# Interleaving the weight units of the gate stage one by one, and converting one unit ahead instead of two

## The reference

```python
mod_x = jax.nn.silu(c) @ ada_w[l] + ada_b[l]                     # c: (1, 1024), ada_w: 1024 x 6144
sh1, sc1, g1, sh2, sc2, g2 = jnp.split(mod_x[:, None, :], 6, axis=-1)
...
px = hx @ w_in[l]                                                # gates gx: 2048 of its columns
g = jax.nn.sigmoid(gates + b_gate)
y = g_f * (f_mix @ w_fourier) + g_a * (att @ w_mla_o)
x = x + g1 * (y @ w_out)
```

## Time and profile before

| | us |
|---|---|
| median of three runs | 1771.61 |
| the profiled execution, its own time | 1770.47 |
| its span in the profile | 1768.7 |
| PE busy | 1677.0 (95%) |
| DVE busy | 1200.7 (68%) |
| ACT busy | 871.0 (49%) |
| the gate stage on PE, about | 151 to 247 |

### The profile page before, as it was taken

One profiled execution on the slowest core, in us unless ns is written; L12 is line 12 of the kernel. 1 busy time (PEld: TensorE's weight loads), 2 busy tenths in 40 slices (PEclk: granted clock), 3 DMA queues, 4 the chain that ended last, 5 costly groups with the idle time before them and its releaser, 6 DMA issues.

```text
span 1768.7 us, 18457 instructions
## 1 busy us (share of the span) xinstructions
PE 1677.0 (95%) x7530; PEld 1307.9 (74%) x7530; DVE 1200.7 (68%) x1334; ACT 871.0 (49%) x973; POOL 112.8 (6%) x139
## 2 busy tenths in 40 slices
PE   5999998989899999998999999889999999999994
PEld 2768875658688888886787667768888888888882
DVE  6545857776553434344487675489898989999894
ACT  6423234443342323232533124467888787887872
POOL 0000021000000000000000220020101011110100
PEclk8999998999899999998999998889999999999997
DMA  9106730012122222221221100279999999999983
GB/s 382 57 31 264 271 111 1 0 48 95 72 96 95 96 95 96 96 95 48 96 75 69 48 25 30 96 265 365 374 373 380 371 359 366 361 371 368 382 326 154
DMA packets 54522, 322.77 MB, mean 182 GB/s; under 512 B 12577, under 2 KB 13089, under 8 KB 17826
## 3 DMA queue, kind: packets, MB, share of 16 engines
q1 hardware_dynamic: 42480, 305.81, 45.9%
q0 software_dynamic: 9216, 8.42, 1.4%
q10 hardware_dynamic: 2738, 7.33, 1.1%
HBM read 325.70 MB, written 20.97 MB: 196 GB/s over the span
## 4 chain that ended last, share of the span: by engine, by line
PE 87%; DVE 8%; ACT 2%; DMA 2%; issue 1%; POOL 0%; SPq 0%; DVEq 0%; POOLq 0%; ACTq 0%
PE ps L524 34%; PE ps L1275 18%; PE ps L1302 10%; PE ps L640 3%; PE ps L1164 2%; PE ps L859 2%; PE ps L1261 2%; DVE scr L2242 2%; DVE wlo L1932 1%; PE ps L925 1%; PE ps L673 1%; PE ps L1004 1%; PE ps L962 1%; DMA xT<-in_x 1%; PE ps L743 1%
## 5 line engine op out<-in xcount | busy, mean ns | idle before, releaser
L1932 DVE TENSOR_TENSOR wlo<-raw,whi 128x2048 fp32r<-128x2048 f32 x268 | 606.7, 2284 | 170.2 <-ACT whi L1363 170.0
L1363 ACT ACTIVATE whi<-raw 128x2048 fp32r<-128x2048 f32 x268 | 508.5, 1914 | 208.6 <-PE ps L524 103.2
L524 PE MATMUL ps<-hH,whi 128*128 128x512 f32 x576 | 229.4, 398 | 0.0
L524 PE MATMUL ps<-hL,whi 128*128 128x512 f32 x576 | 227.5, 395 | 0.0
L524 PE MATMUL ps<-hH,wlo 128*128 128x512 f32 x576 | 227.4, 395 | 0.0
L1275 PE MATMUL ps<-whi,xH 128*128 128x512 f32 x512 | 204.2, 399 | 0.0
L1275 PE MATMUL ps<-whi,xL 128*128 128x512 f32 x512 | 201.2, 393 | 0.0
L1275 PE MATMUL ps<-wlo,xH 128*128 128x512 f32 x512 | 200.0, 391 | 0.0
L524 PEld LDWEIGHTS ps<-hH,whi 128*128 128x128 f32 x576 | 108.1, 188 | 26.3 <-issue 0.5
L524 PEld LDWEIGHTS ps<-hH,wlo 128*128 128x128 f32 x576 | 108.1, 188 | 26.2
L524 PEld LDWEIGHTS ps<-hL,whi 128*128 128x128 f32 x576 | 108.2, 188 | 26.1 <-issue 0.5
(11 more groups left out here) (478 smaller groups left out, 2639.8 us busy)
## 6 DMA issues: line engine op xcount, KB each, us to landing
raw<-in_experts SPq DMA_DIRECT2D x192, 1024.0 KB, 7.4
raw<-in_streamed SPq DMA_DIRECT2D x92, 1024.0 KB, 4.8
xT<-in_x SPq DMA_DIRECT2D x1, 2048.0 KB, 17.2
h_scratch<-hN ACTq DMA_DIRECT2D x4, 512.0 KB, 3.3
Y<-y_scratch SPq DMA_DIRECT2D x4, 512.0 KB, 7.8
Y<-y_scratch ACTq DMA_DIRECT2D x4, 512.0 KB, 8.1
out<-xN SPq DMA_DIRECT2D x4, 512.0 KB, 2.6
ctxT<-in_ctx SPq DMA_DIRECT2D x1, 1024.0 KB, 18.7
```

What stands on the lines that cost most here:

```text
L524: ins = e.matmul(o, l, r, start=(i == 0), stop=(i == len(prs) - 1))
L1363: e.activation(u.hi, u.raw, ACT.Copy).then_inc(*p.inc("hi", n, on="hi"))
L1932: e.tensor_tensor(u.lo, u.raw, u.hi.bitcast(F32), ALU.subtract).then_inc(*p.inc("lo", n, on="lo"))
```

## The change

In the list of units, the order before was g0, g1, mod 4 (two units), g2, mod 5 (two), g3, and so on to g7, mod 10, mod 11. Now it is g0, mod 4, g1, mod 5, g2, and so on to g7, mod 11. In iteration i of the gate stage ACT and DVE converted unit g(i+2); now they convert g(i+1), and on DVE this comes ahead of `mod_row(4 + i)` instead of behind it.

```diff
@@ unit_table
-    for i in range(9):
-        if i < 8:
-            wide("g", "w_in", 0, 8, 928 + 256 * i, 1184 + 256 * i)
-        if i:
-            mod(3 + i)
+    for i in range(8):
+        wide("g", "w_in", 0, 8, 928 + 256 * i, 1184 + 256 * i)
+        mod(4 + i)
@@ act_program, stage "gates"
             use(n)
-            if i + 2 < len(U_G):
-                convert(U_G[i + 2])
+            if i + 1 < len(U_G):
+                convert(U_G[i + 1])
             for m in (2 * i, 2 * i + 1):
                 p.wait_ge(*done("pe", "g", m))
```

## The result

The changed kernel took 1801.88 us, median of 4 runs (1798.51 to 1805.34), against 1771.24 us for the kernel before on the same chip (4 runs, 1770.47 to 1772.28). By these medians it is 30.6 us slower. The ratio of the two kernels is 1.0179, 95% interval 1.0163 to 1.0196; it rests on all 11 runs on record of the changed kernel (1798.51 to 1805.61, mean 1802.95), which is why it is a little above the ratio of the two medians. 1800.5 was predicted. The profiled execution took 1802.24 us.

What follows compares the result with a forecast made beforehand. PE bounded the gate stage before; the change closes a 17.72 us cycle against PE's 12.10. Delay 27.4 + clock 1.5 + end 0.1 = +29.0 us, giving 1800.5 us; 8-in-10 range 1794 to 1807.

Steps and rivals of the forecast that it cites:

- What bounds it: Gate stage before the change: PE never waits and needs 12.10 us per gate unit.
- The ring: Gate stage: row, load, ACT rounding, DVE subtraction, next row form a closed cycle of 17.72 us against PE's 12.10.
- The lag: From a row's end on DVE to the gate unit's landing: 7.5 us, bounds 5.05 and 9.3.
- The start: First gate units: g2 lands at 169.5 us, is ready at 173.8, and PE has 0.7 us to spare.
- The pauses: PE waits ahead of g3 to g7: about 4.9 us ahead of g3, 4 to 5 us ahead of the others.
- The clock: PE at half speed after every pause, losing 1.5 us; only the loss behind g7 stays on the path.
- The end: g7 begins at 262.4 us, row 11 ends just when PE asks, `mod_total(11)` ends at 277.5 against 248.54.
- The sum: Whole kernel: 27.4 + 1.5 + 0.1 = +29.0 us, giving 1800.5 us.
- Loads side by side: Rival: a row's second mod unit and the gate unit load in parallel, lag 5.05 us, 1785.9 us; chance 6%.
- Slower landings: Rival: every gate unit's load lands late, lag 9.3 us, 10.8 us more, 1811 us; chance 5%.
- Clock at half for whole units: Rival: PE runs g3 to g7 at half clock, 21.4 us per unit, 1823 us; chance 3%.
- Not slower: Rival: gate loads go out once their own place is free, no closed cycle, PE bounds, 1771.6 us; chance 4%.

Runs made afterwards that it cites:

- experiment 2: Kernel before with its old load list, but from g2 on converting one gate unit ahead, on DVE ahead of the row: 1772.08 us, ratio 1.0001.
- experiment 3: Changed kernel with DVE's subtraction of g(i+1) moved back behind row 4 + i: 1772.79 us, ratio 1.0001.
- experiment 6: Kernel before with two more DVE multiply-adds in each row: 1771.36 us, ratio 0.9995.
- experiment 1: Changed kernel with its new load list, but gate units converted two ahead again, on DVE behind the row: 1809.71 us, ratio 1.0209.
- Experiment 4: Changed kernel with each gate unit's load placed between the two mod units of a row instead of behind both: 1784.64 us, ratio 1.0071.
- Experiment 7: Changed kernel with 16 more matmuls, results overwritten, ahead of PE's wait for each of g3 to g7: 1803.64 us, ratio 1.0166.
- experiment 5: Changed kernel with two more DVE multiply-adds in each row: 1815.97 us, ratio 1.0233.

## Why the prediction was right, and where its terms were off

**What bounds it.** Right: before, PE alone; experiments 2, 3 and 6 changed lead, loads and DVE's work and moved nothing.

**The ring.** Right as a mechanism and in both of its causes (experiments 1 to 3). Row and subtraction are as worked out (6.06 and 2.21 us on the timeline above). The lag, from the end of the row to the landing, was the uncertain term. It measured 7.9, 7.4, 7.9, 7.3, 9.1 and 7.3 us, together 46.8 where 6 x 7.5 = 45.0 was predicted: +1.8. Five of them lie close to the 7.4 to 7.8 that the pairs of the earlier trace rows gave, and one is a slow landing, as that at 215.2 us was. Three lags lie above 7.5, and in each of these turns it was the mod unit ahead that landed late (5.4, 5.4 and 6.4 us after its issue instead of 4.8 to 4.9); the load of g followed it by 2.5 us in every turn. The mean turn was 18.0 us instead of 17.72. Experiment 4 tests the term from the other side: the load released 3.1 us sooner takes the turn to 14.6.

**The start.** g2 landed at 170.0 instead of 169.5 and PE did not have to wait for it (0.3 us to spare instead of 0.7); the first pause came ahead of g3. Right.

**The pauses.** Five, as forecast, of 3.2 to 5.5 us instead of 4 to 5, 20.8 in all.

**The clock.** Right in kind. The first product of g7 took 7.40 us instead of 5.65: 1.75 instead of the 1.5 read from the earlier trace rows. The size is not fixed, though: in experiment 1 the same product lost 2.9 us, and in experiment 4 four pauses of 1.6 to 3.0 us were followed by no loss at all. Experiment 7 shows that the earlier losses are absorbed.

**The end.** g7 began at 264.36 instead of 262.4, and row 11 was done just when PE asked for it:
```profile
275.23 3.11 DVE L1968 SCALAR_TENSOR_TENSOR rst<-raw,sil,rst 128x512 f32<-128x512 f32 x4 [0.59 <-DMA raw<-in_streamed]
```
It ends at 278.34, and `mod_total(11)` begins at 278.66, 0.48 us after the transposes begin, as it did before: the row was in time by 0.3 us. The row's last half had itself waited for its load; a longer row, as in experiment 5, makes this a wait of 2.3 us for `mod_total(11)`.

**The sum.** +31.2 at the marker for +29.0: +1.8 from the lags, +0.2 from a trace that lies that much later before the stage, and +0.3 in g7's products, most of it the clock (the rounding of the terms makes it 2.3 for 2.2). The median is 1801.88 for 1800.5. That the two lie so close owes a little to chance, since the runs of the changed kernel alone spread over 7.1 us.

**The estimate beside the sum.** The prediction also gives a lag of 9.2 us from the 6.15 us and 341 GB/s that the Trainium skill lists for 1 MB ("DMA: Bandwidth & Descriptors", Measured). These two figures do not fit each other, since 1 MB at 341 GB/s is 3.1 us, and the table is headed as one of transfers issued from GpSimd, where here SP issues them. The lag measured 7.3 to 7.9 us in five turns and 9.1 in one; the sum did not use the estimate.

**The rivals.** Loads side by side (lag 5.05): refuted by all six loads. Slower landings (9.3 each time): one of six (9.1). Clock at half for whole units: refuted by the windows, 1.00 again from 198 us on. Not slower: its condition, a landing within 1.9 us of the row's end, never came near.

## What to carry to other kernels

Two reorderings that are each free can close a ring together, so ask of such a change not what each step costs but whether a unit's release, load and conversion now all lie between one step of an in-order engine and its next. The length of that ring against the bound engine's period gives the time in a sum of four terms, each of which could be read or bounded from the trace before. Then look for the cheapest place to open it: here one step of DVE behind the row instead of ahead of it restored the whole 31 us, and one unit moved in the list 20 us of it.

## What was not expected of the hardware

- Two 1 MB loads issued 0.4 us apart on SP's queue: in three of six turns the first landed after 4.8 to 4.9 us, as one that is alone, and the second 6.9 to 7.0 us after its own issue. In two turns it was 5.4 and 7.5, in one 6.4 and 8.6. In all six the second landed some 2.5 us behind the first. Issued 2.2 us apart, the second landed 7.4 to 7.8 us after the issue of the first; here it was 7.3 to 7.4 in the three quick turns, so issuing the second sooner gained 0.5 us at most.
- One of the six pairs is slow in the changed kernel (8.64 us; the first of that pair took 6.4) and two of six in experiment 4 (8.20 and 8.38 us). In the changed kernel and in experiments 1 and 5 it is the fifth load each time (8.64, 8.32 and 8.24 us), in experiment 7 the sixth (8.01), so it hardly looks like chance. What these meet was not settled.
- A pause of 3.16 us with matmuls on both sides (ahead of g7) was followed by matmuls 0.42 us apart (at 265.34 and 265.76 us), at a granted clock of 0.50 from 265.3 to 268 us. A pause of 2.27 us was followed by the same (ahead of g7 in experiment 7, with matmuls end to end up to it: 0.51 from 265.4 to 268 us), and one of 3.00 us in experiment 4 was not (1.00, starts 0.23 to 0.24 us apart). So the length of the pause alone does not decide it; what does was not settled.
- Two executions can differ by some 3 us outside the stage that is looked at: the profiled one of experiment 7 has a span 3.0 us longer than that of the changed kernel though its stage ends 0.4 us sooner. Over 19 runs the kernel before spreads by 7.6 us. For single steps the marker was the sharper measure, above all counted from the first `wf` matmul, which gives 119.37 or 119.38 us for the kernel before and for experiments 2, 3 and 6; for verdicts it was the ratio.
